# Eight layer norms of a fp32 transformer kernel: moments from the raw sums, weight and factor in one operation, X made later

## What is computed

```python
x = layer_norm(ALPHA*x + 0.5*swiglu(x, ffn1...), ln_g[i,0], ln_b[i,0])
y = mixer_ab(x, ...) if i % 2 == 0 else mixer_c(x, ...)
x = layer_norm(ALPHA*x + y, ln_g[i,1], ln_b[i,1])
x = layer_norm(ALPHA*x + 0.5*swiglu(x, ffn2...), ln_g[i,2], ln_b[i,2])
x = x + sigmoid(x @ ple_wg[i] + ple_bg[i]) * (p[i] @ ple_wp[i])

def layer_norm(x, g, b):
    mu = mean(x, -1)
    var = mean(square(x - mu), -1)
    return (x - mu) * rsqrt(var + eps) * g + b
```

## Time and profile before

| what | before |
|---|---|
| median of 3 runs | 2415.53 us (2413.46 to 2417.34) |
| the profiled execution: its time | 2413.82 us |
| its span in the trace | 2412.4 us |
| mean granted TensorE clock | 0.973 of full speed |
| PE busy | 2257.8 us, 94% of the span |
| DVE busy | 1271.6 us, 53% |
| ACT busy | 1074.9 us, 45% |

### The profile page before, as it was taken

One profiled execution on the slowest core, in us unless ns is written; L12 is line 12 of the kernel. 1 busy time (PEld: TensorE's weight loads), 2 busy tenths in 40 slices (PEclk: granted clock), 3 DMA queues, 4 the chain that ended last, 5 costly groups with the idle time before them and its releaser, 6 DMA issues.

```text
span 2412.4 us, 39225 instructions
## 1 busy us (share of the span) xinstructions
PE 2257.8 (94%) x17014; PEld 2017.2 (84%) x17014; DVE 1271.6 (53%) x1928; ACT 1074.9 (45%) x1691; POOL 54.2 (2%) x100
## 2 busy tenths in 40 slices
PE   6999979998999999989996989999999999998997
PEld 5998869997999799879995766888888886477997
DVE  3555566556555666365555326763444653446665
ACT  3444455445444554354435526552333451345553
POOL 0000100000000000000000000000000000000000
PEclk9999989999999999989998999999999999999998
DMA  7454625545554544245444121022223433204451
GB/s 313 175 192 184 228 107 206 195 170 197 185 200 166 205 188 166 108 183 189 183 158 193 70 74 49 1 105 87 88 101 126 158 123 136 74 18 156 165 200 39
DMA packets 51627, 353.58 MB, mean 147 GB/s; under 512 B 8064, under 2 KB 8448, under 8 KB 8832
## 3 DMA queue, kind: packets, MB, share of 16 engines
q1 hardware_dynamic: 47520, 346.05, 38.4%
q10 hardware_dynamic: 864, 4.63, 0.5%
q0 software_dynamic: 3072, 0.40, 0.1%
HBM read 349.61 MB, written 1.05 MB: 145 GB/s over the span
## 4 chain that ended last, share of the span: by engine, by line
PE 85%; DVE 8%; ACT 4%; DMA 1%; issue 1%; SPq 0%; POOL 0%; DVEq 0%; ACTq 0%
PE ps L683 13%; PE ps L685 13%; PE ps L684 13%; PE ps L818 5%; PE ps L2381 5%; PE ps L2383 5%; PE ps L2382 4%; PE ps L383 3%; PE ps L384 2%; PE ps L385 2%; PE ps L2111 2%; PE ps L2112 2%; PE ps L2113 2%; PE ps L1347 1%; PE ps L884 1%; PE ps L871 1%
## 5 line engine op out<-in xcount | busy, mean ns | idle before, releaser
L358 DVE TENSOR_TENSOR wl<-ring,wh 128x1024 fp32r<-128x1024 f32 x406 | 477.5, 1221 | 276.0 <-ACT wh L353 275.4
L683 PE MATMUL ps<-xs,wh 128*128 128x256 f32 x1760 | 504.5, 287 | 24.8 <-DVE wl L358 13.9
L684 PE MATMUL ps<-xs,wl 128*128 128x256 f32 x1760 | 503.2, 286 | 0.0
L685 PE MATMUL ps<-xs,wh 128*128 128x256 f32 x1760 | 503.1, 286 | 0.0
L353 ACT ACTIVATE wh<-ring 128x1024 fp32r<-128x1024 f32 x406 | 405.1, 1050 | 177.8 <-PE ps L685 128.0
L683 PEld LDWEIGHTS ps<-xs,wh 128*128 128x128 f32 x1760 | 343.6, 195 | 28.3 <-issue 18.9
L684 PEld LDWEIGHTS ps<-xs,wl 128*128 128x128 f32 x1760 | 343.4, 195 | 0.0
L685 PEld LDWEIGHTS ps<-xs,wh 128*128 128x128 f32 x1760 | 343.2, 195 | 0.0
L683 PE MATMUL ps<-hh,wh 128*128 128x256 f32 x880 | 249.1, 283 | 0.7 <-DVE hl L784 0.7
L684 PE MATMUL ps<-hh,wl 128*128 128x256 f32 x880 | 249.0, 283 | 0.0
L685 PE MATMUL ps<-hl,wh 128*128 128x256 f32 x880 | 249.0, 283 | 0.0
(11 more groups left out here) (426 smaller groups left out, 4004.5 us busy)
## 6 DMA issues: line engine op xcount, KB each, us to landing
ring<-wstream SPq DMA_DIRECT2D x329, 1024.0 KB, 4.9
ada_rows<-ada_stage POOLq DMA_DIRECT2D x96, 4.0 KB, 4.3
CN<-consts ACTq DMA_DIRECT2D x1, 1136.0 KB, 15.7
X<-xin ACTq DMA_DIRECT2D x1, 1024.0 KB, 10.7
X<-cin ACTq DMA_DIRECT2D x1, 1024.0 KB, 9.2
out<-X SPq DMA_DIRECT2D x1, 1024.0 KB, 3.9
PT__65<-pin ACTq DMA_DIRECT2D x1, 512.0 KB, 18.9
ab_w<-wab ACTq DMA_DIRECT2D x1, 512.0 KB, 3.7
```

Of the source, the lines that this page charges most:

```text
L358: dve.tensor_tensor(lo, tile_of(i), hi.bitcast(F32), ALU.subtract).then_inc(low_part, 1)
L683: pe.matmul(out, wh[:, w, c, :], x_hi, start=start, stop=False, skip_group_check=True)
L684: pe.matmul(out, wl[:, w, c, :], x_hi, start=False, stop=False, skip_group_check=True)
L685: return pe.matmul(out, wh[:, w, c, :], x_lo, start=False, stop=True, skip_group_check=True)
```

## The change

In the eight norms the mean and the mean square are both taken from the raw sums in Z. ACT squares a pair of chunks as soon as Z has it. PE takes the squares of the first four chunks one by one, between the pair sums of the mean, and those of the last four in two pairs that DVE adds. ACT squares the mean, DVE subtracts that from the mean square (L657), and Ln and Exp follow. The mean is still subtracted from Z, by `dve_less_mean`, which no longer has to be done before the squares. In the six norms of the first stack one operation multiplies Z by weight and rstd (`dve_gained`), and another adds the bias and subtracts the high part (`dve_low_of_gained`); X itself is made later, from Z and the bias (`dve_x`), and only where it is read: `ffn1_0`, `ffn2_0`, `ffn1_1`, `ffn2_1`. Behind `ab` and `c` the residual is made from Z, by eight operations on ACT with ALPHA times the bias. The table load is the first thing of ACT's norm, both pieces of PE's other work come behind the matmuls of the norm, and the first half of the projection on ACT moves behind the norm.

```diff
+        def pe_moments(name):
+            i, (sums, sq) = LNS.index(name), ln_scratch(name)
+            for q in range(4):
+                pe.wait_ge(z_paired, 4 * i + q + 1)
+                mm = pe.matmul(row(4), mean, sums[:, q, :], start=(q == 0), stop=(q == 3))
+                if q < 2:
+                    pe.wait_ge(squared, 4 * i + q + 1)
+                    for c in (2 * q, 2 * q + 1):
+                        pe.matmul(row(5), mean, sq[:, c, :], start=(c == 0), stop=False)
+            mm.then_inc(mean_done, 1)
+            for q in (2, 3):
+                pe.wait_ge(two_squares, 2 * MOMENTS.index(name) + q - 1)
+                mm = pe.matmul(row(5), mean, sq[:, 2 * q, :], start=False, stop=(q == 3))
+            mm.then_inc(var_done, 1)
         def pe_layer_norm(name, fill=(None, None)):
-            pe_mean(name)
-            if fill[0]:
-                fill[0]()
-            pe_variance(name)
-            if fill[1]:
-                fill[1]()
+            pe_moments(name)
+            for work in fill:
+                if work:
+                    work()
...
+        def dve_gained(name, q):
...
+                dve.scalar_tensor_tensor(z, z, pcol(LN_GB[name][0], c), rstd[:, 0:T], ALU.mult,
+                                         ALU.mult).then_inc(z_gained, 1)
+        def dve_low_of_gained(name, q):
...
+                low = dve.scalar_tensor_tensor(xs[:, c, 1, :], Z[:, 0, c, :], pcol(LN_GB[name][1], c),
+                                               xs[:, c, 0, :].bitcast(F32), ALU.add, ALU.subtract)
+        def dve_x(name):
+            dve.wait_ge(z_gained, 8 * LNS.index(name) + 8)
+            for c in range(KC):
+                dve.tensor_scalar(X[:, 0, c, :], Z[:, 0, c, :], pcol(LN_GB[name][1], c), None, ALU.add).then_inc(x_done, 1)
...
+        def dve_moments(name, ahead=()):
+            i = MOMENTS.index(name)
+            for t in ahead[0:1]:
+                dve_low(t)
+            dve_square_pair(name, 2)
+            dve_square_pair(name, 3)
+            for t in ahead[1:2]:
+                dve_low(t)
+            dve.wait_ge(square_of_mean, i + 1)
+            dve_less_mean(name, 0)
+            dve.wait_ge(var_done, LNS.index(name) + 1)
+            dve.tensor_tensor(lnv[:, 0:T], row(5), rstd[:, 0:T], ALU.subtract).then_inc(var_ready, 1)
+            dve_less_mean(name, 1)
+            dve_less_mean(name, 2)
+        def dve_norm_to_parts(name, ahead=()):
+            dve_moments(name, ahead)
+            dve_gained(name, 0)
+            dve_less_mean(name, 3)
+            dve_low_of_gained(name, 0)
+            dve_gained(name, 1)
+            dve_gained(name, 2)
+            dve_low_of_gained(name, 1)
+            dve_gained(name, 3)
+            dve_low_of_gained(name, 2)
+            dve_low_of_gained(name, 3)
...
+        def act_moments(name):
+            for q in range(4):
+                act_square(name, q)
+            act.wait_ge(mean_done, LNS.index(name) + 1)
+            act.activation(rstd[:, 0:T], row(4), ACT.Square).then_inc(square_of_mean, 1)
...
+        def act_residual_of_gained(name):
...
+            for c in range(KC):
+                z = act.activation(Z[:, 0, c, :], Z[:, 0, c, :], ACT.Identity, scale=ALPHA, bias=ln_eps[:, at + c:at + c + 1])
...
         def act_mixer_ab():
             t0 = TILE0["ab_in"]
+            act_high(t0 + 2)
             act.wait_ge(*x_normed("ffn1_0"))
             act.dma_start(ab_w[:, :, :], wab).then_inc(in_wab, 16)
-            act_high(t0 + 2)
             act_scale("ab")
...
             for t in range(12):
                 if t + 2 < 12:
                     dve_low(t0 + t + 2)
+                if t == 0:
+                    dve_x("ffn1_0")
```

More of the change, by code:

```diff
@@ L192 @@
 LN_BANKS = {"l0_1c": (0, 1), "l0_2x": (0, 1)}
+LN_LATE = LNS[6:]
+MOMENTS = LNS[0:6] + LNS[10:12]
+CENTRED = LNS[6:10]
+LN_GB = {name: (f"ln_g{k // 3}{k % 3}", f"ln_b{k // 3}{k % 3}") for k, name in enumerate(LNS[0:6])}
 LN_COLS = ["l0_1", "l0_2", "l1_1"]
-X_MADE = ["ffn1_0", "ab", "ffn2_0", "ffn1_1", "c", "ffn2_1", "l1_2"]
+X_MADE = ["ffn1_0", "ffn2_0", "ffn1_1", "ffn2_1", "l1_2"]
+LN_AB = {"ffn2_0": ("ab", 2), "ffn2_1": ("c", 10)}
 X_AFTER = {"ffn1_0": "ab", "ab": "ffn2_0", "ffn2_0": "ple0", "ffn1_1": "c", "c": "ffn2_1", "ffn2_1": "ple1",
@@ L753, in act_ffn @@
                 if src is None:
-                    act.wait_ge(*x_normed({"ffn2_0": "ab", "ffn2_1": "c"}[name]))
-                act_scale(name)
+                    act_residual_of_gained(name)
+                else:
+                    act_scale(name)
             act_high(i0 + 5)
@@ L1259, in dve_ple @@
                 dve_low(t0 + t)
+            dve_x(f"ffn2_{i}")
+            dve.wait_ge(*x_normed(f"ffn2_{i}"))
             for t in range(8):
@@ L1890, in dve_mixer_c @@
             dve.memset(c_eps[:, 1:2], P * 1e-12).then_inc(*c_gate_v("eps"))
+            dve_x("ffn1_1")
             dve_low(t0 + 2)
@@ L2891, in act_program @@
             act_ffn(0, "ffn1_0", X[:, 0])
-            act.wait_ge(eps_set, 1)
-            act_layer_norm("ffn1_0", ("ln_g00", "ln_b00"), 64, ahead=tiles("ab_in"))
+            act.wait_ge(eps_set, 3)
+            act_layer_norm("ffn1_0", 64, ahead=tiles("ab_in"))
             act_mixer_ab()
-            act_layer_norm("ab", ("ln_g01", "ln_b01"), 128, ahead=tiles("ffn2_0"))
+            act_layer_norm("ab", 128, ahead=tiles("ffn2_0"))
             act_ffn(1, "ffn2_0", None, ahead=2)
-            act_layer_norm("ffn2_0", ("ln_g02", "ln_b02"), ahead=tiles("ple_g_0"),
-                           beside=lambda: act_ple_proj(0, 0))
+            act_layer_norm("ffn2_0", ahead=tiles("ple_g_0"))
             act_ple(0, "ffn2_0")
@@ L2901, in act_program @@
             act_ffn(2, "ffn1_1", X[:, 0], copies=168)
-            act_layer_norm("ffn1_1", ("ln_g10", "ln_b10"), 192, ahead=tiles("c_k"))
+            act_layer_norm("ffn1_1", 192, ahead=tiles("c_k"))
             act_mixer_c()
-            act_layer_norm("c", ("ln_g11", "ln_b11"), 344, ahead=tiles("ffn2_1"))
+            act_layer_norm("c", 344, ahead=tiles("ffn2_1"))
             act_ffn(3, "ffn2_1", None, ahead=2)
-            act_layer_norm("ffn2_1", ("ln_g12", "ln_b12"), ahead=tiles("ple_g_1"),
-                           beside=lambda: act_ple_proj(1, 0))
+            act_layer_norm("ffn2_1", ahead=tiles("ple_g_1"))
             act_ple(1, "ffn2_1")
@@ L2950, in dve_program @@
             dve_odd_mixer()
-            dve_layer_norm("l1_1", None, tiles("l1"))
+            dve_norm_to_modulated("l1_1", tiles("l1"))
             dve_ffn(5, "l1", None, lambda c: MOD[:, 1, 40 + c, 0:1], conv=1, ahead=2)
-            dve_layer_norm("l1_2")
+            dve_moments("l1_2")
+            dve_less_mean("l1_2", 3)
+            for q in range(4):
+                dve_scaled("l1_2", q)
             for c in range(1, KC, 2):
-                dve.wait_ge(z_normed, 4 * LNS.index("l1_2") + c // 2 + 1)
+                dve.wait_ge(z_normed, 4 * LN_LATE.index("l1_2") + c // 2 + 1)
                 dve.tensor_scalar(X[:, 0, c, :], Z[:, 0, c, :], pcol("l1_ln2g", c), pcol("l1_ln2b", c), ALU.mult,
```

131 lines of the change are left out of this document (83 added, 48 removed).

## The result

| | before | changed |
|---|---|---|
| median of 4 runs | 2414.49 us | 2391.61 us (2389.27 to 2394.99) |
| the profiled execution | 2413.82 us | 2394.99 us |
| its span | 2412.4 us | 2393.7 us |
| ratio to before | | 0.9913 (95%: 0.9899 to 0.9927) |

The change is 0.87% faster by the ratio, 22.9 us by the medians, where 10.3 were forecast and the range ended at 2399.5. The ratio's own interval reaches from 18 to 24 us.

What follows compares the result with a forecast made beforehand. PE, busy 94% of the span, was taken as the bound, so DVE and ACT edits pay only where PE waits, as in norms. Eight items sum to -10.3 us from 2413.82; 1.7 added for the median gives 2405.2 us, range 2399.5 to 2411.0.

Steps and rivals of the forecast that it cites:

- Item 2: Norm `ab`: arrivals 1.4 us earlier, but the residual as eight operations ends 0.7 us later and delays a tile; -0.6 us.
- Rival C: The waits behind the norms are smaller than worked out: 4.3 us more gain, 2401 us; chance 0.13.
- The norm itself: In `ffn1_0` the second low part ends 3.8 us earlier, the first input arrival comes 1.9 us earlier, the last 2.5.
- The price of a three-operand operation: DVE's 16 such operations in a norm take a pitch of 0.40 us each, with bounds of 0.34 and 0.69.
- rival A: Three-operand operations run at half rate, 0.69 us each, making six norms longer: 2428 us; chance 0.04.
- B: Rival: gains ahead of the first product are absorbed by waits behind it; gain 5.4 us, 2410 us; chance 0.24.
- D: Rival: PE's clock stays low another 2 us in six norms, costing 6 us; 2413 us with B's gain; chance 0.02.
- Item 1: Behind `ffn1_0` two tiles end about 2 us earlier, but the fourth waits behind X and the residual on ACT; +0.8 us.
- Items 3 and 6: `ffn2_0` and `ffn2_1`: PE's projection ends sooner without the variance in between, two tiles run without pause; -2.7 us each.
- Item 4: Norm `ffn1_1`: the first two tiles end 1.5 us earlier and X is done barely before; -1.5 us.
- Items 5 and 7: `c` and `l1_1`: sums come late, single squares delay the mean and eat the gain; +0.4 and +0.3 us.
- Item 8: Last norm `l1_2`, where nothing hides anything: from the mean to the last X 7.1 us instead of 11.4; -4.3 us.

Runs made afterwards that it cites:

- e7: The kernel before with four useless matmuls between the pair sums of the norm `ab`; ratio to before 1.0006.
- e4: The change with the four single squares behind the mean's four matmuls instead of between them, in all eight norms; ratio to before 0.9915.
- e6: The change with the first piece of PE's other work back between the mean and the paired squares, in five norms; ratio to before 0.9929.
- e9: The change with ACT's table load put back behind the squares, in all norms; ratio to before 0.9953.
- e2: The change's moments in all eight norms, with weight, bias, X and residual as in the kernel before; ratio to before 0.9923.
- e8: The change with e5's edit, and the single squares behind the mean in `ffn1_0`, `ffn1_1`, `c` and `l1_1` alone; median 2385.74 us, ratio to before 0.9887.
- e3: The kernel before with only its last norm, `l1_2`, as in the change; ratio to before 0.9985.
- e10: The kernel before with one line of the change alone, the table load as the first thing of ACT's norm, in all norms; ratio to before 0.9960.
- e5: The change with ACT making the fourth weight tile's high part before it waits for X, behind `ffn1_0`; ratio to before 0.9903.
- e1: The changed kernel run again without an edit; median 2392.57 us, ratio to before 0.9918.

## Why the prediction was wrong

The direction and the place were right: the gain lies in the path from the last pair sum to rstd, and the table load, the second weight tile and the centring are what left it. The size was less than half of the measured one by the medians. By its steps:

- **Item 2: the step that failed most, by 2.4 us in both traces.** Two terms were wrong. The arrivals were put 1.4 us earlier, with the low clock of the trace before kept in the changed norm; the first came 3.0 us earlier. The single squares fill PE's pauses and hold the clock, which is 0.3 to 0.5 us of it (e7, e4); the rest is the shorter chain. And the residual's eight operations, priced by rows with a column as factor (4.03 us), were to make a tile wait. They take 494 ns each, 3.29 us together, no tile waits for them, and the tail is 191.2 us before and after. Rival C had this.
- **The norm itself: mis-sized.** rstd was put at 6.4 us behind the last pair sum and came at 5.88; the first low part at 9.1, and it came at 8.33. ACT's square of the mean starts 0.2 us sooner than forecast, and the high part behind it starts 0.28 us after it and not 0.5, so that the second low part ends 0.5 us sooner. Some 0.7 us are missing for this wherever the first product waits for the input. How much of it reached the whole no run shows.
- **The price of a three-operand operation**: right. The pitch of 0.40 us is that of the row (0.88 for two), 479 ns each. The half rate of rival A (0.69) is not there. Nor did B or D come: no matmul in the 30 us behind the first product of `ffn2_0` waits, and over the 30 us behind the last pair sum of the seven norms ahead of the last the granted clock was 0.85 to 1.00 before and 0.89 to 1.00 after. (D's 2413 is also added up wrongly: 2405.2 and 6 and the 4.9 of B make 2416.)
- **Item 1: the number came out by luck.** The wait ahead of the fourth tile was there, by the chain that the item names, but that chain began 1.5 us sooner than forecast (X was done 17.2 us behind the last pair sum, forecast 18.7). So the tile started 0.8 us sooner than before and not 0.8 later. The +0.8 of the first trace is made behind it, by the clock that fell after the wait: 1.5 us until the fifth tile. The prediction did not have that, and the second trace has +1.7.
- **Items 3 and 6**: their mechanism held (two tiles without a pause). The third tile starts 3.4 us sooner in both, for 2.7. The place of the projection, which the item names, is 0.9 to 1.0 of that (e6); the table load, put back, costs 1.1 to 1.2 there (e9), the three-operand operations left out 0.9 (e2).
- **Item 4**: at the end of the first two tiles it gave 2.6 to 3.1 us for 1.5. What is left of it at the end of the stage is not to be told, since the mixer c varies by 10 us with the clock.
- **Items 5 and 7: wrong sign.** "That eats the gain" let the mean's delay of 1.7 us take all of it. The norms still gained 0.9 and 0.6 us, since the centring, the squares and the table load had left the path behind the mean. That the delay itself was real, and avoidable, e4 and e8 show. Beyond its 0.6 us the stage of `l1_1` tells nothing, with -1.6 in one trace and -0.1 in the other.
- **Item 8**: right, 4.5 for 4.3, and e3 shows it alone.
- **What no item held**: 3.4 us between the change's profiled execution and its median, 0.7 on the other side, and 1.6 in untouched stages, which the second trace does not have.

With its own numbers the prediction should have seen that both queues, ACT's and DVE's, lead to rstd one to one, and priced the table load apart: this one line is 8 to 10 us of the 20 in the changed kernel (e9), and 5 to 10 put into the kernel before (e10). What stays open is 1 to 6 us: the intervals of the norms and tails, without the mixer c, sum to 19 us in the first trace of the change and 15 in the second, and the ratios say 20 to 21, with intervals that reach down to 18 and 15.

## What to carry to other kernels

Before you price a clever rewrite, price each thing that stands in the same queue ahead of the value that all wait for: a table load moved to the front was a quarter to a half of this gain. Where an engine idles ahead of an operation, ask what its own earlier work was holding up elsewhere; in e9 the idle time of 2.23 us was no cover for the load. Where runs scatter by more than the effect, measure it as an interval between two instructions of the trace: in most norms here it repeats to 0.02 us, where the ratios leave 3 open. But let the interval reach to where the last arrival has been used: the first product showed little or nothing of what e2, e6 and e9 did behind `ffn2_0`. And a term that comes out at the right number is not yet right: item 1 had its +0.8 from another cause.

## What the runs showed of the hardware

- A pause of PE can cost again after it. In the mixer ab an idle of 1.9 us was followed by a granted clock of 0.70 over 5 us, and both went together with the wait (e5): 2.4 to 3.3 us in all. A wait of 0.90 us in the same place (e6) was not followed by a fall. Useless matmuls in the pauses between sums held the clock at 1.00 where it fell to 0.50 without them (e7).
- On ACT, 128x256 with a column for the factor and one for the bias took 587 ns, with a constant factor or none and a column for the bias 494.
- A three-operand operation of DVE with one column took 479 ns at 128x256 with two float32 sources in SBUF, against 420 without a column. The Trainium skill (Vector Engine (DVE) Microarchitecture Reference, Points that are easy to get wrong) says half throughput for two such sources; no row here shows that; by an estimate from the 512-element rows of 0.69 us, that would be its price.
- The same program ran between 2388.9 and 2403.8 us (e1), with a mean granted clock of 0.978 in the shortest run and 0.971 in the longest. The mixer c alone took 231 and 235 us in the two traces of the change, and 225 to 235 over all.
